# Which places of a weight ring the cross-attention's key and value pieces take, and a DRAM buffer per layer for keys and values

## What is computed

```
x = x + 0.5 * swiglu_ffn(rms_norm(x))                     # ffn1
proj = rms_norm(x) @ w_mix_in                             # 1024 -> 3328
x = x + concat(rwkv7(proj...), moba_attention(proj...)) @ w_mix_out
mem_n = rms_norm(mem, mem_norm_g[l])                      # 256 memory tokens
q = rms_norm(x) @ w_q ;  k, v = split(mem_n @ w_kv)       # 1024 -> 2048
x = x + softmax(q k^T / 16) v @ w_o                       # cross-attention
x = x + 0.5 * swiglu_ffn(rms_norm(x))                     # ffn2
```

## Time and profile before

| | before |
|---|---|
| median of 3 runs | 2267.16 us |
| the profiled execution | 2264.74 us, of it the span of instructions 2262.9 us |
| TensorE matmuls busy | 2182.5 us, 96% of the span |
| VectorE busy | 1240.8 us, 55% |
| ScalarE busy | 424.7 us, 19% |
| mean granted TensorE clock | 0.998 of full speed |
| moved by DMA | 499.94 MB, mean 221 GB/s |

### The profile page before, as it was taken

One profiled execution on the slowest core, in us unless ns is written; L12 is line 12 of the kernel. 1 busy time (PEld: TensorE's weight loads), 2 busy tenths in 40 slices (PEclk: granted clock), 3 DMA queues, 4 the chain that ended last, 5 costly groups with the idle time before them and its releaser, 6 DMA issues.

```text
span 2262.9 us, 29955 instructions
## 1 busy us (share of the span) xinstructions
PE 2182.5 (96%) x12564; PEld 1481.2 (65%) x12564; DVE 1240.8 (55%) x2258; ACT 424.7 (19%) x852; POOL 47.5 (2%) x79
## 2 busy tenths in 40 slices
PE   7999999999999889999999999999999999999998
PEld 5778853333333338857978768857884966687873
DVE  2798432100011146667576766676666867667675
ACT  1123321100000012101232321102210132322110
POOL 1000100000000000000000000000000000000000
PEclk9999999999999999999999999999999999999999
DMA  9656579999999985444341435436443441245441
GB/s 406 266 225 257 223 212 381 422 421 421 422 422 421 422 323 174 161 167 171 123 154 50 149 126 182 155 124 223 161 175 130 168 150 57 78 150 183 159 181 42
DMA packets 174716, 499.94 MB, mean 221 GB/s; under 512 B 7016, under 2 KB 99448, under 8 KB 144384
## 3 DMA queue, kind: packets, MB, share of 16 engines
q1 hardware_dynamic: 170416, 481.23, 56.4%
q0 software_dynamic: 4032, 16.43, 2.3%
q10 hardware_dynamic: 144, 0.52, 0.1%
HBM read 491.34 MB, written 6.82 MB: 220 GB/s over the span
## 4 chain that ended last, share of the span: by engine, by line
PE 84%; DMA 12%; DVE 2%; issue 1%; ACT 0%; SPq 0%; POOL 0%; DVEq 0%; POOLq 0%
PE bank L2487 23%; PE bank L2535 11%; DMA ring<-in_w 10%; PE bank L939 6%; PE bank L2600 6%; PE bank L1512 6%; PE bank L3030 2%; PE bank L1553 2%; PE bank L2848 2%; PE bank L3103 2%; PE bank L2705 2%; PE bank L1602 1%; PE bank L2711 1%; PE bank L929 1%; PE bank L1043 1%; PE bank L1074 1%
## 5 line engine op out<-in xcount | busy, mean ns | idle before, releaser
L2487 PE MATMUL bank<-Tw,Sx 128*128 128x256 f32 x1032 | 229.9, 379 | 0.0
L2487 PEld LDWEIGHTS bank<-Tw,Sx 128*128 128x128 f32 x1032 | 193.0, 190 | 24.6
L1969 DVE TENSOR_TENSOR sg<-sg,bank 128x512 f32<-128x512 f32 x16 | 11.0, 687 | 273.7 <-PE bank L1512 273.7
L2487 PE MATMUL bank<-ring,xT 128*128 128x256 f32 x688 | 155.5, 379 | 0.0
L2487 PEld LDWEIGHTS bank<-ring,xT 128*128 128x128 f32 x688 | 130.5, 190 | 18.0 <-issue 0.5
L939 PE MATMUL bank<-xT,ring 128*128 128x256 f32 x640 | 141.8, 380 | 0.0
L1512 PE MATMUL bank<-ring,xg 128*64 128x512 f32 x512 | 115.0, 595 | 23.7 <-DMA ring<-in_w 23.7
L939 PEld LDWEIGHTS bank<-xT,ring 128*128 128x128 f32 x640 | 120.7, 190 | 19.0 <-issue 3.3
L1512 PE MATMUL bank<-more,xg 128*64 128x512 f32 x512 | 115.1, 596 | 16.8 <-DMA more<-in_w 16.0
L1553 PE MATMUL bank<-ring,hTg 128*64 128x512 f32 x512 | 113.5, 595 | 0.0
L3527 DVE TENSOR_TENSOR whole<-bank,part 128x256 f32<-128x256 f32 (+1 forms) x133 | 57.4, 432 | 99.4 <-PE bank L2487 98.1
(11 more groups left out here) (640 smaller groups left out, 3679.2 us busy)
## 6 DMA issues: line engine op xcount, KB each, us to landing
ring<-in_w SPq DMA_DIRECT2D x128, 1024.0 KB, 23.6
ring<-in_ffn_w_in SPq DMA_DIRECT2D x88, 1024.0 KB, 7.7
ring<-in_first_pieces SPq DMA_DIRECT2D x33, 2048.0 KB, 12.8
more<-in_w SPq DMA_DIRECT2D x64, 1024.0 KB, 23.5
ring<-in_ffn_w_out SPq DMA_DIRECT2D x20, 2048.0 KB, 7.8
ring<-in_w_mix_in SPq DMA_DIRECT2D x12, 2048.0 KB, 7.8
ring<-in_xattn_w_kv SPq DMA_DIRECT2D x6, 2048.0 KB, 8.0
ring<-in_w_mix_out SPq DMA_DIRECT2D x4, 2048.0 KB, 15.9
```

Of the source, the lines that this page charges most:

```text
L2487: last = nc.tensor.matmul(bank[BANK_OF[name]][:, 0:SEQ], lhs(k), rhs(k), start=(k == 0), stop=(k == 3))
```

## The change

The remaining groups of a layer are no longer tied to the pieces of their own columns: groups LEFT[l][2n] and LEFT[l][2n+1] use the nth w_kv place. Layer 0 fills places 24, 25 and 26 and skips 27 (before it skipped 26); layer 1 fills 24 and 25 and skips 26 and 27 (before it skipped 24 and 25). `read`, `skipped`, the list of columns to load and `cross_kv`'s wait follow from that. The number of loads, their sizes and the matmuls stay. In DRAM each layer gets its own key and value buffer; the early keys of layer 1 go straight to that layer's.

```diff
--- before.py
+++ after.py
@@ -155,7 +155,7 @@
     _full.append(_s)
     _at = _s[1]
 EARLY_SEGMENTS = [_s for _s in _full if _s[0] < _s[1]]
-EARLY_COLUMNS = [(_l, _g * 256 if _g < 4 else D + 512 + (_g % 2) * 256) for _l, _g, _ in EARLY]
+EARLY_COLUMNS = [(_l, _g * 256 if _g < 4 else D + (_g // 2 - 2) * 512 + (_g % 2) * 256) for _l, _g, _ in EARLY]
 EARLY_LAYERS = list(dict.fromkeys(_l for _l, _, _ in EARLY))
 
 
@@ -593,10 +593,9 @@
         xsm = sb("xsm", [16], xat)
         xat.close()
         ph2.close()
-        k_dram = nc.dram_tensor("cross_keys", (P, KD * SEQ), F32)
-        k_early = nc.dram_tensor("early_keys", (P, KD * SEQ), F32)
-        v_dram = nc.dram_tensor("cross_values", (P, NT * D), F32)
-        v_rows = v_dram.ap().rearrange("p (t d) -> p t d", t=NT)
+        k_dram = [nc.dram_tensor(f"cross_keys{l}", (P, KD * SEQ), F32) for l in range(DEPTH_2)]
+        v_dram = [nc.dram_tensor(f"cross_values{l}", (P, NT * D), F32) for l in range(DEPTH_2)]
+        v_rows = [v_dram[l].ap().rearrange("p (t d) -> p t d", t=NT) for l in range(DEPTH_2)]
         bias_dram = nc.dram_tensor("bias_by_distance", (NH, P, NDIST), F32)
 
 
@@ -822,16 +821,16 @@
             pool.dma_start(gup[:, :], a["rwkv_g_up_2"][0]).then_inc(lc_loaded, 16)
             pool.dma_start(late_gain, a["mem_g_late"]).then_inc(early_moved, 16)
             pool.wait_ge(kv_act, 2)
-            pool.dma_start(v_rows[:, :, 0:512], v_out[:, :, 0:512]).then_inc(v_stored, 16)
+            pool.dma_start(v_rows[0][:, :, 0:512], v_out[:, :, 0:512]).then_inc(v_stored, 16)
             pool.wait_ge(bd_stored, 16)
             pool.wait_ge(v_stored, 16)
             for u, (l, g, _) in enumerate(EARLY):
                 pool.wait_ge(early_act, u + 2 + EARLY_LAYERS.index(l))
-                if l == 1:
-                    pool.dma_start(k_early.ap()[:, g * 512:(g + 1) * 512], flat(early_out)).then_inc(early_moved, 16)
+                if g < 4:
+                    pool.dma_start(k_dram[l].ap()[:, g * 512:(g + 1) * 512], flat(early_out)).then_inc(early_moved, 16)
                 else:
-                    c = 512 + (g % 2) * 256
-                    pool.dma_start(v_rows[:, :, c:c + 256], early_out).then_inc(early_moved, 16)
+                    c = (g // 2 - 2) * 512 + (g % 2) * 256
+                    pool.dma_start(v_rows[l][:, :, c:c + 256], early_out).then_inc(early_moved, 16)
 
 
         def tensor1(pe):
@@ -2040,7 +2039,6 @@
 
 
         J_SKIPPED = (51,)
-        J_VALUES = J_KV + 2
         assert PER_LAYER % SLOTS == 0 and J_MIX == FB + N_DOWN
 
         def slot_of(j):
@@ -2052,7 +2050,7 @@
         LEFT = [[g for g in range(8) if cross_left(l, g)] for l in range(DEPTH_2)]
         KV_DONE = [2 + sum(len(t) for t in LEFT[:l + 1]) for l in range(DEPTH_2)]
         KEYS_LEFT = [sum(g < 4 for g in t) for t in LEFT]
-        assert all(n in (0, 4) for n in KEYS_LEFT)
+        assert all(t[0::2] == [g - 1 for g in t[1::2]] for t in LEFT)
 
         def keys_stored(l):
             return 16 * sum(1 for m in range(l + 1) if KEYS_LEFT[m])
@@ -2061,8 +2059,7 @@
             return 16 * (1 + sum(1 for m in range(l + 1) if len(LEFT[m]) > KEYS_LEFT[m]))
 
         def skipped(l, j):
-            return (j in J_SKIPPED or (l, j) == (0, J_VALUES)
-                    or J_KV <= j < J_KV + 4 and not any(cross_left(l, g) for g in (2 * (j - J_KV), 2 * (j - J_KV) + 1)))
+            return j in J_SKIPPED or J_KV + len(LEFT[l]) // 2 <= j < J_KV + 4
 
         def transfers(l, j):
             if skipped(l, j):
@@ -2369,7 +2366,7 @@
                         sp.wait_ge(proj_full, mx_done(l, n if n < 5 else MX_UNITS, "P3"))
                     sp.sem_inc(sp_passed, 1)
                 elif j < J_MIXOUT:
-                    sp.wait_ge(kv_psum, kv_done(l, 2 * (j - J_KV) + 1))
+                    sp.wait_ge(kv_psum, kv_done(l, LEFT[l][2 * (j - J_KV) + 1]))
                     sp.sem_inc(sp_passed, 1)
                 elif j < J_XQ:
                     sp.wait_ge(out_psum, mo_done(l, ("P2", "P3")[j - J_MIXOUT]))
@@ -2384,7 +2381,8 @@
             for l in range(DEPTH_2):
                 ffn(l, 0)
                 mid = [(a["w_mix_in_2"], 512 * n, 512 if n < 6 else 256) for n in range(7)]
-                mid += [(a["xattn_w_kv_2"], 512 * n, 512) for n in range(4)]
+                mid += [(a["xattn_w_kv_2"], 512 * (LEFT[l][2 * n] // 2 if 2 * n < len(LEFT[l]) else 0), 512)
+                        for n in range(4)]
                 mid += [(a["w_mix_out_2"], 512 * n, 512) for n in range(2)]
                 mid += [(a["xattn_w_q_2"], 512 * n, 512) for n in range(2)]
                 mid += [(a["xattn_w_o_2"], 512 * n, 512) for n in range(2)]
@@ -2409,22 +2407,24 @@
                 norm_rstd(pool, l * 4 + 4)
                 norm_rstd(pool, l * 4 + 5)
 
-                if KEYS_LEFT[l]:
-                    pool.wait_ge(kv_act, kv_done(l, 3))
+                keys, values = LEFT[l][:KEYS_LEFT[l]], LEFT[l][KEYS_LEFT[l]:]
+                if keys:
+                    pool.wait_ge(kv_act, kv_done(l, keys[-1]))
                     pool.sem_inc(pool_passed, 1)
-                    pool.dma_start(k_dram.ap(), flat(k_out[:, :, :])).then_inc(k_stored, 16)
-                if len(LEFT[l]) > KEYS_LEFT[l]:
-                    pool.wait_ge(kv_act, kv_done(l, 7))
+                    pool.dma_start(k_dram[l].ap()[:, keys[0] * 512:(keys[-1] + 1) * 512],
+                                   flat(k_out[:, 2 * keys[0]:2 * keys[-1] + 2, :])).then_inc(k_stored, 16)
+                if values:
+                    pool.wait_ge(kv_act, kv_done(l, values[-1]))
                     pool.sem_inc(pool_passed, 1)
-                    columns = slice(512 if l == 0 else 0, D)
-                    pool.dma_start(v_rows[:, :, columns], v_out[:, :, columns]).then_inc(v_stored, 16)
+                    columns = slice((values[0] // 2 - 2) * 512, (values[-1] // 2 - 1) * 512)
+                    pool.dma_start(v_rows[l][:, :, columns], v_out[:, :, columns]).then_inc(v_stored, 16)
                 pool.wait_ge(k_stored, keys_stored(l))
                 pool.wait_ge(v_stored, values_stored(l))
                 pool.wait_ge(early_moved, 16 + 16 * len(EARLY))
                 pool.wait_ge(ycat, (l + 1) * 2)
                 pool.sem_inc(pool_passed, 1)
-                pool.dma_start(flat(kx[:, :, :]), (k_dram if KEYS_LEFT[l] else k_early).ap()).then_inc(kv_loaded, 16)
-                pool.dma_start(flat(vx[:, :, :]), v_dram.ap()).then_inc(kv_loaded, 16)
+                pool.dma_start(flat(kx[:, :, :]), k_dram[l].ap()).then_inc(kv_loaded, 16)
+                pool.dma_start(flat(vx[:, :, :]), v_dram[l].ap()).then_inc(kv_loaded, 16)
                 norm_rstd(pool, l * 4 + 6)
                 norm_rstd(pool, l * 4 + 7)
 
@@ -2697,7 +2697,7 @@
                     else:
 
                         pe.wait_ge(kv_act, kv_done(l, LEFT[l][nth - 2]))
-                s = wait_piece2(pe, J_KV + g // 2, l)
+                s = wait_piece2(pe, J_KV + LEFT[l].index(g) // 2, l)
                 w = slot_w(s, KD, 512)
                 if g >= 4:
                     t = g % 2
```

## The result

The change makes the kernel slower. Eleven runs of the changed kernel have a median of 2271.88 us (2269.42 to 2276.18), eleven of the kernel before 2266.98 us (2261.84 to 2269.9). The ratio is 1.0027, 95% interval 1.0019 to 1.0035, so +6.1 us (+4.3 to +7.9 us). The forecast was 2263.8 us in a range of 2256.4 to 2269.6 us.

A forecast was written before the change was run, and what follows sets the result against it. TensorE, busy 96% of the span, was taken as the bound. Wait 2.53 plus clock 1.67 made 4.2 us, cut by VectorE to 3.4; other terms 0: 2267.16 - 3.4 = 2263.8 us, range 2256.4 to 2269.6.

The forecast's parts named there:

- part 1: Layer 1's w_kv loads, in places 24 and 25, land before TensorE asks, so its 2.53 us wait goes.
- the clock (1.67 us): Layer 1's first remaining value group runs slowly because the clock falls after the wait; removing the wait regains 1.67 us.
- the limit by VectorE: Layer 1: VectorE's own chain up to `fac_ready` and `turned(0)` cuts TensorE's gain from 4.2 to 3.4 us.
- rival 1: The clock part in layer 1 isn't regained, leaving a gain of 2.5 us: 2264.7 us, chance 0.25.
- part 2: Layer 1's w_mix_out and both layers' first w_q loads, released later, still arrive before use: cost 0.
- The prediction's own sign of it: The forecast is wrong if TensorE's idle time put down to issue grows in the inversions; no size given.
- rival 2: Load bursts at the inversions' start starve TensorE of instructions in both layers, losing 10.1 us: 2273.9 us, chance 0.10.
- Part 3: Layer 1's 1 MB value store meets two 2 MB loads but lands before ScalarE needs it: 0 us.
- Part 4: A DRAM key and value buffer per layer changes only addresses: 0 us, with 1.5 us either way in the range.

The follow-up runs named there:

- experiment 12: The kernel before, with layer 0's first w_q piece held until the last inversion step, so 4 MB go out together behind the inversions: 1.0005, 2267.72 us.
- experiment 1: The changed kernel with the w_kv pieces back in their old places, leaving only the DRAM buffer per layer: 0.9993 against the kernel before, 2263.66 us.
- experiment 3: The changed kernel with layer 0's places put back, so only layer 1 has the new places 24 and 25: 1.0016 against the kernel before, 2268.35 us.
- experiment 5: The kernel before, with layer 0's second w_mix_out piece and first w_q piece held until value group 7, the inversions' start: 1.0016, 2269.53 us.
- experiment 6: The kernel before, with only layer 0's first w_q piece held until the second of five inversion steps has ended: 1.0012, 2268.18 us.

## Why the prediction was wrong

**Right: the wait, its cause and its removal (part 1).** The pieces are issued at the ends of units 3 and 4 (SyncE at 1817.63, which is 32.5 us ahead of `rwkv_operands`, and again 12.5 us later), the wait and its row are gone.

**Right for this execution, overrated for the median: the clock (1.67 us) and the limit by VectorE.** With the old places the stretch from `rwkv_operands` to `turned(0)` takes 35.8 to 36.0 us in four of nine executions and 34.2 to 34.4 us in the other five. Two of them beside each other, with the fallen clock (experiment 12) and without (experiment 1):

```profile
1849.71 8.80 PE L2708 MATMUL bank<-ring,gm 128*128 128x512 f32 x16 [2.55 <-DMA ring<-in_xattn_w_kv]
```

```profile
1848.52 7.11 PE L2707 MATMUL bank<-ring,gm 128*128 128x512 f32 x16 [2.44 <-DMA ring<-in_xattn_w_kv]
```

The wait is the same; after it the clock falls in some executions and stays in others. With the new places it is 32.4 to 32.5 us in all five that have them. So the gain is 3.5 us where the clock fell and 1.8 us where it didn't, 2.6 us on average. The page "TensorE: Matmul & The Clock Gate" of the Trainium skill, whose run-to-run rule I set beside the sum and put into rival 1, was right. The rival's price, 2.5 us, was still too high: VectorE takes 0.5 us of it at `fac_ready` and some more at `turned(0)` in that case too.

**Wrong: part 2, "cost 0" for the loads that are released later.** The cover was worked out rightly, nobody waited for w_mix_out or w_q. The step that failed is the question itself: a load was priced by who needs it, not by what it keeps from passing. The prediction's own sign of it came: TensorE's idle time put down to issue grew from 1.9 to 6.9 us. The loads left stretches in which TensorE takes few instructions (11 per us in 1166 to 1196 of the kernel before, where w_q's first piece of layer 0 was issued) and went into the one in which it takes the most. Measured: 5.6 us in layer 1 (mean of the change and experiment 3) and 1.8 to 4.2 us in layer 0.

**Wrong: the weight of rival 2.** It named the place, the mechanism and nearly the price (10.1 us of loss; the stretches give 5.6 + 3.0 = 8.6 us), and got a chance of 0.10. That the price is so near is partly luck: it was worked out as half pace for as long as a burst lasts, and TensorE kept its pace and then stood still. What spoke against it was TensorE busy in 3.00 of 3.00 us beside the store. That row covers the first 3 us; in the changed kernel the first stop comes at 1209.39, 8.4 us after the load was issued, when what TensorE had in stock is used up (521 matmuls and weight loads since the last packet's start). Whoever reads busy time right behind a burst's start sees the stock. And the store was 1 MB, where 5.2 MB were to come.

**Part 3** priced the meeting of store and loads by ScalarE's wait for the store. That wait did not appear, as forecast. **Part 4**, 0 us, was right (experiment 1).

**The sum as it should have been:** -2.6 + 5.6 + 3.0 = +6.0 us, against +6.1 us (4.3 to 7.9) by the ratio and +4.9 us by the medians. Each of the two losses is the mean of two single executions, so that the match is this close is luck in part.

**What stays open.** The traces show the instruction packets late and the stops behind them, and that a burst needs a high rate of instructions and no write to SBUF to do harm. Where a packet is held up is narrowed but not shown: once started, the late packets of the table take 0.9 to 1.1 us, no longer than others (0.9 to 1.4 us in the inversions of the kernel before), so the delay lies ahead of their start. Whether busy DMA engines or busy DRAM cause it stays open. How much of layer 1's loss is the standing still and how much the clock behind it was not separated.

## What to carry to other kernels

A load whose data is needed late is not free wherever it is put: before moving a transfer, read how many instructions the engines take in the new stretch (here 73 per us in the inversions, 26 behind) and keep bursts of 2 MB and more out of the dense one. When slots of a ring are given out anew, list every piece whose release changes, not only the one that is to come earlier; places 24 and 27 give the gain without a new burst, 0.9988 (0.9978 to 0.9999), and beat both kernels. And a cost seen in one execution that hangs on the clock, such as the 1.67 us here, should be entered with its frequency: it came in four of nine.

## What the hardware showed that I had not expected

- TensorE can run out of instructions while nothing in the program makes it wait. The profile puts it down to "issue": 2.59 us and 2.27 us in one piece, 8.4 and 5.4 us behind the issue of loads of 2 and 4 MB. What it has in hand in the inversions is some 500 matmuls and weight loads, 7 us of work (521 and 507 between two packets' starts in the two layers of the change, 517 in experiment 5). The Trainium skill, page "Runtime: NRT & Kernel Launch", section "Instruction fetch mechanics", has instructions fetched in blocks of 16 KiB, as here (1.47 MB in 90 packets), and calls the cost of a block's boundary mostly hidden. In this kernel that holds outside the inversions and not beside a burst inside them (28 of 29 stops end 1.3 to 1.6 us behind a packet's landing); there the measurement decides.
- The clock can fall behind such a stop: 0.50 in 1914 to 1916, behind 2.27 us of standing still. Behind 2.59 us in layer 0 and behind 3.18 us in experiment 6 it stayed at 1.00.
- A copy within DRAM can stop TensorE as a weight load does: 2.6 us in three stops in the one execution traced.
